# Sums over partitions in a two-model transformer kernel: from a one-column TensorE product to VectorE's block turn and row sums

## The reference

```python
for l in range(DEPTH):                                  # DEPTH = 2
    mod = jax.nn.silu(c) @ w_ada[l] + b_ada[l]          # (1,1024) @ (1024,3072) + (3072)
    shift, scale, gate = jnp.split(mod, 3, axis=-1)
    h = x * (1.0 + scale[:, None, :]) + shift[:, None, :]
    ...
    x = layer_norm_2(ALPHA * x + (1.0 + gate[:, None, :]) * sub, ln_g[l], ln_b[l])
```

## Time and profile before

| | us |
|---|---|
| median of 3 runs (1319.64 to 1320.63) | 1320.0 |
| the profiled execution | 1319.7 |
| its span in the profile | 1317.9 |
| TensorE busy in it | 1298.7 |
| VectorE busy | 1044.3 |
| ScalarE busy | 679.9 |
| GpSimd busy | 105.7 |

### The profile page before, as it was taken

The page is one execution under the profiler, slowest core; times in us unless marked ns, Lnnn a source line. Parts: engine busy times, 40 slices in busy tenths (PEclk is TensorE's granted clock), DMA queues, the critical chain, the costliest instruction groups (busy, mean ns, idle before and its releaser), DMA issues.

```text
span 1317.9 us, 18920 instructions
## 1 busy us (share of the span) xinstructions
PE 1298.7 (99%) x6968; PEld 1095.1 (83%) x6968; DVE 1044.3 (79%) x1689; ACT 679.9 (52%) x1101; POOL 105.7 (8%) x153
## 2 busy tenths in 40 slices
PE   9999999999999999999999999999999999999997
PEld 7788888788888888888887888888889998798995
DVE  6688778887888777878788887888767798966987
ACT  6444444744544444444537435444445767457672
POOL 1011100011011001101010011111000000000000
PEclk9999999999999999999999999999999999999999
DMA  8988856527888857888756349888656463464630
GB/s 266 341 268 281 265 186 208 145 95 240 273 270 270 258 191 233 274 267 274 231 168 215 102 155 326 270 300 271 204 180 191 140 221 129 144 215 132 192 129 33
DMA packets 218093, 281.73 MB, mean 214 GB/s; under 512 B 19793, under 2 KB 159185, under 8 KB 217489
## 3 DMA queue, kind: packets, MB, share of 16 engines
q1 hardware_dynamic: 183248, 223.12, 52.3%
q0 software_dynamic: 11712, 40.60, 9.2%
q10 hardware_dynamic: 23040, 16.79, 4.0%
HBM read 271.00 MB, written 9.46 MB: 213 GB/s over the span
## 4 chain that ended last, share of the span: by engine, by line
PE 88%; DVE 6%; DMA 3%; ACT 1%; issue 1%; SPq 1%; DVEq 0%; ACTq 0%
PE ps L836 27%; PE ps L838 26%; PE ps L837 26%; PE ps L920 3%; DMA w_raw<-in_ffn_w_gu 3%; DVE w_lo L1364 2%; PE ps L1070 2%; PE ps L1105 1%; PE ps L1131 1%; DMA w_raw<-in_w_in 1%; DVE few_first L1393 1%; DVE y L1392 1%; PE ps L1039 0%; PE ps L1117 0%; ACT w_hi L1162 0%
## 5 line engine op out<-in xcount | busy, mean ns | idle before, releaser
L1364 DVE TENSOR_TENSOR w_lo<-w_raw,w_hi 128x1024 fp32r<-128x1024 f32 (+2 forms) x420 | 495.4, 1212 | 73.5 <-ACT w_hi L1162 71.1
L1162 ACT ACTIVATE w_hi<-w_raw 128x1024 fp32r<-128x1024 f32 (+2 forms) x420 | 432.5, 1053 | 233.7 <-DMA w_raw<-in_ffn_w_gu 94.0
L836 PE MATMUL ps<-w_hi,col_hi 128*128 128x512 f32 (+2 forms) x1024 | 396.9, 388 | 3.9 <-DVE w_lo L1364 2.1
L838 PE MATMUL ps<-w_hi,col_lo 128*128 128x512 f32 (+2 forms) x1024 | 392.0, 383 | 0.0
L837 PE MATMUL ps<-w_lo,col_hi 128*128 128x512 f32 (+2 forms) x1024 | 391.7, 383 | 0.0
L836 PEld LDWEIGHTS ps<-w_hi,col_hi 128*128 128x128 f32 x1024 | 192.5, 188 | 47.8 <-DVE w_lo L1364 4.1
L838 PEld LDWEIGHTS ps<-w_hi,col_lo 128*128 128x128 f32 x1024 | 192.4, 188 | 38.6
L837 PEld LDWEIGHTS ps<-w_lo,col_hi 128*128 128x128 f32 x1024 | 192.6, 188 | 34.9
L836 PE MATMUL ps<-w_hi,lat_hi 128*128 128x512 f32 (+2 forms) x544 | 208.8, 384 | 0.0
L838 PE MATMUL ps<-w_hi,lat_lo 128*128 128x512 f32 (+2 forms) x544 | 206.5, 380 | 0.0
L837 PE MATMUL ps<-w_lo,lat_hi 128*128 128x512 f32 (+2 forms) x544 | 206.3, 379 | 0.0
(11 more groups left out here) (153 smaller groups left out, 1171.6 us busy)
## 6 DMA issues: line engine op xcount, KB each, us to landing
w_raw<-in_ffn_w_gu SPq DMA_DIRECT2D x352, 256.0 KB, 4.9
w_raw<-in_w_in SPq DMA_DIRECT2D x108, 512.0 KB, 4.6
w_raw<-in_ffn_w_down SPq DMA_DIRECT2D x88, 512.0 KB, 5.5
mod<-in_w_ada POOLq DMA_DIRECT2D x32, 768.0 KB, 6.9
w_raw<-in_w_out SPq DMA_DIRECT2D x24, 512.0 KB, 4.5
hidden_blocks<-arena ACTq DMA_DIRECT2D x32, 256.0 KB, 5.7
arena<-hidden_blocks ACTq DMA_DIRECT2D x128, 64.0 KB, 4.2
norm_g<-in_ln_g POOLq DMA_DIRECT2D x8, 512.0 KB, 4.1
```

What stands on the lines that cost most here:

```text
L836: pe.matmul(dst, a_hi, b_hi, start=start, stop=False)
L838: return pe.matmul(dst, a_lo, b_hi, start=False, stop=stop)
L1162: act.activation(half_of(w_hi[j], n, h), half_of(raw[j], n, h), ACT.Copy).then_inc(hi_ready, 1)
L1364: tt(half_of(w_lo[j], n, h), half_of(raw[j], n, h), half_of(w_hi[j], n, h).bitcast(F32), ALU.subtract)\
```

## The change

The sum over the 128 partitions is no longer a product on TensorE. `modsplit` and `spread` are gone. Instead:

- `modturn` (VectorE, at the place of `modsplit`): a block transpose of `ada_sum`, each 32x32 block in itself, and a sum along the rows of 32. After it, partition 32a + t holds for column 32b + t the sum over the 32 partitions of group a, as six values b (`ada_part`).
- `modmove` (ScalarE, at the place of `spread`, one round later): four copies of 32 partitions x 6 that bring the four groups to partitions 0 to 31, side by side (`ada_parts`).
- `modrow` (VectorE): one sum over the four parts and the bias, which lies beside them as a fifth. It stands at another place: behind the down product of its round, just ahead of `modturn`, where before it stood ahead of `modsum`. GpSimd's part of it moves with it in the list.
- The row is now 32 partitions x 6 values, and so the bias is loaded and the result stored in single values of 4 bytes.

```diff
     for r in range(2, ROUNDS):
         jobs += gu(r, 0)[:1] + stored(r - 1) + gu(r, 0)[1:] + by_pe(r - 1) + parts(r - 2)
         if r > 2:
-            jobs += [("spread", s, r - 3), ("modrow", s, r - 3)]
+            jobs += [("modmove", s, r - 3)]
         if r < 2 + MOD_STEPS:
             jobs += [("modsum", s, r - 2)]
         jobs += gu(r, 1)[:1] + moved(r - 1) + gu(r, 1)[1:] + blocks(r)
         if lag < ROUNDS - TAIL:
             jobs += down(lag, 0) + down(lag, 1)
             lag += 1
+        if r > 2:
+            jobs += [("modrow", s, r - 3)]
         if r < 2 + MOD_STEPS:
-            jobs += [("modsplit", s, r - 2)]
+            jobs += [("modturn", s, r - 2)]
...
-                elif kind == "spread":
-                    b, m = TURN[job][0]
-                    pe.wait_ge(mod_lo, at["modsplit", ("modsplit", s, job[2])])
-                    pe.wait_ge(free[b], m)
-                    pe.matmul(ps[0:1, 7, 0:2 * MOD_W], ones[:, 0:1], ada_both[:, :], start=True, stop=True).then_inc(turned[b], 1)
...
-                elif kind == "modsplit":
-                    act.wait_ge(mod_summed, at["modsum", ("modsum", s, job[2])])
-                    act.activation(ada_hi, ada_sum, ACT.Copy).then_inc(mod_hi, 1)
+                elif kind == "modmove":
+                    act.wait_ge(mod_folded, at["modturn", ("modturn", s, job[2])])
+                    if at["modmove", job] > 1:
+                        act.wait_ge(mod_row, at["modmove", job] - 1)
+                    for a in range(4):
+                        act.activation(ada_parts[:, a, :], ada_part[32 * a:32 * a + 32, :], ACT.Copy).then_inc(mod_moved, 1)
...
-                elif kind == "modsplit":
-                    dve.wait_ge(mod_hi, at["modsplit", job])
-                    tt(ada_lo, ada_sum, ada_hi.bitcast(F32), ALU.subtract).then_inc(mod_lo, 1)
+                elif kind == "modturn":
+                    nth = at["modturn", job]
+                    dve.wait_ge(mod_summed, at["modsum", ("modsum", s, job[2])])
+                    dve.transpose(ada_turned, ada_sum.rearrange("p (b t) -> p b t", t=32)).then_inc(mod_turned, 1)
+                    dve.wait_ge(mod_turned, nth)
+                    if nth > 1:
+                        dve.wait_ge(mod_moved, 4 * (nth - 1))
+                    dve.tensor_reduce(ada_part, ada_turned, AX_X, ALU.add).then_inc(mod_folded, 1)
                 elif kind == "modrow":
-                    b, n = TURN["spread", s, job[2]][0]
                     dve.wait_ge(bias_in, at["bias_in", ("modsum", s, job[2])])
-                    dve.wait_ge(turned[b], n + 1)
-                    steps.wait(tt(ada_row, ps[0:1, 7, 0:MOD_W], ada_bias, ALU.add))
-                    tt(ada_row, ada_row, ps[0:1, 7, MOD_W:2 * MOD_W], ALU.add).then_inc(mod_row, 1)
-                    dve.wait_ge(mod_row, at["modrow", job])
-                    dve.sem_inc(free[b], 1)
+                    dve.wait_ge(mod_moved, 4 * at["modmove", ("modmove", s, job[2])])
+                    dve.tensor_reduce(ada_row, ada_parts.rearrange("p a b -> p b a"), AX_X, ALU.add).then_inc(mod_row, 1)
...
-                pool.dma_start(ada_bias, t["b_ada_2"][l, cols].partition_broadcast(1)).then_inc(bias_in, 16)
+                pool.dma_start(ada_parts[:, 4, :], t["b_ada_2"][l, cols].rearrange("(b t) -> t b", t=32),
+                               allow_slow_non_contiguous=True).then_inc(bias_in, 16)
...
-                    pool.dma_start(mod_rows[l, cols].partition_broadcast(1), ada_row).then_inc(mod_stored, 16)
+                    pool.dma_start(mod_rows[l, cols].rearrange("(b t) -> t b", t=32), ada_row,
+                                   allow_slow_non_contiguous=True).then_inc(mod_stored, 16)
```

More of the change, by code:

```diff
@@ L408, in turn_banks_of @@
     kind, s = job[:2]
-    return {"xt": ((job[-1] + (job[2] if s == 0 else 0)) % 2 if kind == "xt" else 0,), "ht": (0,), "spread": (1,), "tr": (0, 1), "turn": (0, 1),
+    return {"xt": ((job[-1] + (job[2] if s == 0 else 0)) % 2 if kind == "xt" else 0,), "ht": (0,), "tr": (0, 1), "turn": (0, 1),
             "trret": (job[-1] % 2,) if kind == "trret" else (), "trlat": (job[-1] % 2,) if kind == "trlat" else (),
@@ L515, in count_jobs @@
             COUNT.add("y_ready", (s, job[2], job[3]))
-        if kind in ("latent", "sq", "rope", "rot", "idx", "idxw", "ropeA", "ropeK", "modsum", "modsplit", "modrow"):
+        if kind in ("latent", "sq", "rope", "rot", "idx", "idxw", "ropeA", "ropeK", "modsum", "modturn", "modmove", "modrow"):
             COUNT.add(kind, job)
@@ L675, in build @@
         ada_sum = mod[:, KT * MOD_W:(KT + 1) * MOD_W]
-        ada_row = mod[0:1, (KT + 1) * MOD_W:(KT + 2) * MOD_W]
-        ada_bias = mod[0:1, (KT + 2) * MOD_W:(KT + 3) * MOD_W]
-        ada_both, _ = sb("ada_both", [P, 2 * MOD_W], F32R, mod_at + 4 * (KT + 3) * MOD_W)
-        ada_hi, ada_lo = ada_both[:, 0:MOD_W], ada_both[:, MOD_W:2 * MOD_W]
+        ada_turned = mod[:, (KT + 1) * MOD_W:(KT + 2) * MOD_W].rearrange("p (b t) -> p b t", t=32)
+        o = (KT + 2) * MOD_W
+        ada_part = mod[:, o:o + 6]
+        ada_parts = mod[0:32, o + 6:o + 36].rearrange("p (a b) -> p a b", a=5)
+        ada_row = mod[0:32, o + 36:o + 42]
         mod_rows = nc.dram_tensor("mod_rows", (DEPTH, MOD), F32, kind="Internal").ap()
```

4 lines of the change are left out of this document (2 added, 2 removed).

## The result

The changed kernel takes **1590.4 us** (median of 4 runs, 1585.9 to 1595.7) against 1320.0 for the kernel before, measured beside it: a ratio of **1.205, interval 1.203 to 1.207**, slower. The forecast was 1465 with a range of 1425 to 1525: the sign and the mechanism came out, the size did not. The loss is 270 us where 145 was expected. By the prediction's own sign, a landing of the store of 7 us or more, it is the small pieces that were priced too low; the landing is 7.7 us. The profiled execution took 1585.9 us, 1584.1 of it span. In the changed kernel the chunk's weights are requested at line 1740, the row is stored at 1780 and the bias requested at 1744; 1479 begins `modsum`, 1496 is `modrow`, 839 to 841 are the three passes of a product.

A forecast was written before the change was run, and what follows sets the result against it. TensorE, busy 99%, bounds the kernel before; the later modrow makes VectorE's modsum wait in a loop through memory. 1319.7 + 142 (stalls in four stages) + 4 (clock) - 1 (removed products) = 1465 us, range 1425 to 1525.

The forecast's parts named there:

- The bound and the mechanism: TensorE bounds the kernel before; the later modrow delays the chunk's weights, so modsum waits in 24 of 32 chunks.
- The formula: Loss in the four ffn stages: 4 x (L - 6.6 + 5 x (L - 7.34) - 5.3), or 24 L - 194 us.
- L: Chain from the end of modrow through store, landing and bias issue to the landed next chunk, put at 14.0 us.
- The small pieces, 0.4 us: Bias and result moving as 192 pieces of 4 bytes, not sixteen of 48, add 0.4 us to the chain.
- small pieces are slow: Rival: 192 small pieces cost 4 us more in landing and issue, L = 18, 1561 us; chance 8%.
- The store's landing at the new place, 4.64: GpSimd's wait for the stored row to land, 4.64 us, taken from the kernel before.
- The chunk's landing, 6.4: Landing of the next chunk's weights, 6.4 us, a third of the way from the median 6.9 to the least 5.3.
- The lead, 5.3 us: Time from the first splits behind modsum to TensorE's use of that weight half: 5.3 us of lateness hidden per stage.
- The clock, 4 us: Slower matmuls behind the last stall of each stage after the clock falls: 0 to 13 us in all, 4 taken.
- the lateness is not taken back: Denies the rival that VectorE recovers each round and the stall does not feed itself: 48 us, 1368 us; chance 5%.
- a clock that stays low: Rival: the clock does not return between gaps, TensorE is the bound again, 389 us more, 1709 us; chance 5%.
- the first rival: No stall: the chunk lands in time, TensorE stays the bound and gains 6.4 us, 1313 us; chance 4%.

The follow-up runs named there:

- late_only: The kernel before, with its product and 48-byte pieces, and only modrow moved to the later place: 1429.9 us, ratio 1.084.
- after_24: The changed kernel with VectorE's turn reading at a stride of six, so store and bias go in 32 pieces of 24 bytes: 1431.8 us, ratio 1.086.
- late_store_pieces: late_only with the store alone cut into 192 pieces of 4 bytes from one partition's row, VectorE's sums reordered to match: 1602.0 us, ratio 1.215.
- load_before_landing: The changed kernel, but GpSimd requests the weights of chunk c + 2 behind the store's issue and ahead of the wait for its landing: 1480.3 us, ratio 1.122.
- keep_clock: The changed kernel with spare TensorE products, 36 ahead of the wait of rounds 5 to 9 and 48 ahead of round 9's hidden-row turn: 1556.9 us, ratio 1.179.
- early_row: The changed kernel with modrow back at its old place just ahead of modsum, small pieces kept: 1326.8 us, ratio 1.0085.
- early_pieces: The kernel before, modrow at its old place, with only store and bias load cut into 192 pieces of 4 bytes: 1327.7 us, ratio 1.0065.
- load_first: The changed kernel, but GpSimd requests the next chunk's weights right behind modsum, ahead of the wait for the previous modrow and its store: 1377.5 us, ratio 1.044.
- early_24: early_row with VectorE's turn reading at a stride of six, so store and bias go in 32 pieces of 24 bytes: 1312.3 us, ratio 0.9949.
- freed_24: both_freed with store and bias in 32 pieces of 24 bytes instead of 192 of 4: 1312.2 us, ratio 0.9946.
- late_both_pieces: late_store_pieces with the bias load cut into 192 pieces of 4 bytes too: 1608.6 us, ratio 1.220.
- both_freed: load_first, with the bias also requested right behind the store's issue instead of behind its landing: 1352.0 us, ratio 1.024.

## Why the prediction was wrong, step by step

**The bound and the mechanism: right.** TensorE's chain gave way to the loop modsum, modrow, store, landing, bias, weights, landing, modsum. modsum waits in exactly 24 chunks; VectorE's part of the loop is 9.2 us to the tenth in the turn shown (1052.63 to 1061.83); there are gaps ahead of the first product behind the low halves, and the clock falls. The formula, fed with each kernel's own landings, holds over the whole range:

| kernel | issues and gaps + store wait + chunk = L | by the formula | further terms | measured loss |
|---|---|---|---|---|
| late_only | 2.6 + 2.5 + 7.3 = 12.4 | 103 | two sums 12 | 110 |
| after_24 | 2.7 + 2.1 + 7.7 = 12.5 | 106 | | 113 |
| the changed kernel | 2.67 + 7.87 + 7.9 = 18.4 | 248 | bias 23 | 270 |
| late_store_pieces | 2.7 + 7.5 + 8.0 = 18.2 | 242 | two sums 19, bias 19 | 283 |
| load_before_landing | 2.1 + 0 + 11.7 = 13.8 | 137 | bias 25 | 161 |

The sum is within 7 us of each. The tighter lead, below, would add 12 to all five and put the sums up to 17 us above the measured loss, so a part of the close fit is luck. The loop and its factor of 24 hold; what failed first is L.

**The small pieces, 0.4 us: the step that failed.** I scaled from the load of c, 1,024 pieces that landed in 5.5 us, and took a fifth of the difference, by the number of pieces (192 to 1,024). That row was a poor neighbour on two counts. It is a read from DRAM, and the term on the path is a write to DRAM: in keep_clock the same 192 pieces of 4 bytes land in 2.3 us as the load of the bias and in 7.1 us as the store. And nothing showed that the excess grows in proportion to the number. The runs show 2.0 to 7.4 us for the store alone at the same place (late_only, late_store_pieces), and 7.7 to 1.6 back again (the changed kernel, after_24): 5.4 to 6.1 us, 130 to 146 us of time. The rival "small pieces are slow" was the case that came true, with 8% and a price of 4 us. L came out at 18.4 where it said 18, and that is partly luck: the pieces cost more than its 4 us, and the rest of the chain less than was taken. Its time, 1561, lacks the bias. What spoke for giving it more was in the prediction itself: it said that no row showed a store in such pieces, and its price was then bounded from above by rows of a load.

**Number or size of the pieces.** The prediction took the number of pieces to be what would matter, since by the Trainium skill ("DMA: Bandwidth & Descriptors", Specifications) 48 and 4 bytes both fall under the 512 below which a transfer is done as read-modify-write. 16 pieces of 48 bytes landed in 2.0 us, 32 of 24 in 1.6 and 192 of 4 in 7.2 to 7.7 at the later place. Being under 512 bytes is thus not enough to make a store slow. Whether the number or the size does it is not shown: both change together, and no run holds one of them fixed.

**The store's landing at the new place, 4.64: too long by 2.** In late_only it is 2.5 a time. At the later place the store falls into a stall, when less is under way: over the landings of its 32 stores the DMA engines are busy 0.33 in late_only and 0.87 in the kernel before (medians of windows of 2.0 and 4.3 us). A landing read in a full round did not hold there. I had argued so for the chunk ("fewer rounds in a given time") and not for the store.

**The chunk's landing, 6.4: too short.** 7.3 to 7.9. The argument for going below the median of 6.9, that the DMA engines have less to do, fails: they have less to do over a round, but not during this load, when they are full (1.07 in the window above, 1.00 to 1.06 over three such loads in the kernel before). Why the load takes longer than 6.9 us in late_only, at 0.94 to 0.96, stays open. Of the difference 0.2 to 0.6 us is the small pieces (7.7 in after_24 and 7.3 in late_only against 7.9). The errors of the store and of the chunk cancel in part: without small pieces L is 12.4 to 12.5 where I had 13.6, and the range given covers the 1430 of late_only.

**The lead, 5.3 us.** For the first product behind modsum it holds. But a tighter reader stood in round 10: the turn of the hidden rows of round 9 (`ht`, line 923), which needs a hidden product that stands behind modsum, and waits 50.4 us in 4. The kernel before, VectorE and TensorE at that place:

```profile
935.04 0.41 DVE L1453 SCALAR_TENSOR_TENSOR arena<-arena,ps 128x256 f32<-128x256 f32 x1
```

```profile
937.68 0.60 PE L920 MATMUL ps<-ident,arena 128*128 128x128 f32 x4
```

That is 937.68 - 935.45 = 2.2 us. I had looked only at the parts of the hidden blocks and taken them to be no tighter; this reader is, by about 3 us a stage. It is also the largest of TensorE's added waits in early_row (7.3 us in 4) and early_pieces (4.3 in 4), which lose time with waits of modsum of only 1 to 2 us; the kernel before has none there. In late_only the one-column product is one more such reader: it waits 39.3 us in 21 for `modsplit`, which now stands behind modrow.

**The bias in round 10: missing.** 23.0 us in 4 waits. The bias is requested behind the same landing as the weights, and I had followed only the weights. In load_first it is the second loop.

**The clock, 4 us: not settled.** The clock falls behind the gaps and comes back. In the turn shown, behind a gap of 4.41 us, TensorE's products start 0.43 us apart (1058.91, 1059.34), and soon 0.23 apart again (1062.00, 1062.23). TensorE's busy time rose from 1298.7 to 1354.3 us although 32 products are gone; how much of that stood on the path is not shown. keep_clock is 33 us faster, but moved the transfers too, and the sums in the table above reach the measured loss without a term for the clock. So my 0 to 13 us is neither confirmed nor refuted; spare products long enough to hold the clock and short enough not to end the round were not tried.

**The other rivals: out.** modsum waits in 24 chunks, so there is a stall. In rounds 4 to 9 modrow follows modrow by 24 to 30 us, not by 16.5, so the lateness is not taken back: the stall does feed itself. The clock returns within the round, and the time is not the 1709 of a clock that stays low.

**The removed products, 6.4 us: right.** They could not be seen in the changed kernel; early_24 and freed_24 gain 6.4 to 6.5 us, on 1312 where the first rival had 1313. **VectorE's and ScalarE's new work: right,** no cost; VectorE's sums are 0.19, 0.36 and 0.35 us, against 0.2 and twice 0.352 taken.

## What to carry to other kernels

Before a wait is placed later in an in-order queue, follow everything that the other queues have behind it, and read each reader of the late data, not the first one: a loop through memory turns one microsecond into as many as it has turns. When data is rearranged between engines, choose the order of the elements by the transfer at the end; a stride in VectorE's read made its turn 0.16 us longer (0.51 against 0.355), on an engine with time to spare, and turned 192 pieces into 32. And where no row shows a form of transfer, its bound is not the nearest row of another direction: let the range reach as far as the rival that names it.

## What the runs showed of the hardware

- A store of 768 bytes to DRAM by GpSimd's queue lands in 1.6 us as 32 pieces of 24 bytes (after_24), 2.0 as 16 of 48 (late_only), and 7.2 to 7.7 as 192 of 4 (late_both_pieces, late_store_pieces, the changed kernel), at the same place of the program. At the old place it is 3.7 (early_24), 4.3 (the kernel before), and 8.2 to 8.5 (early_pieces, early_row).
- With 192 pieces it takes 6.7 us even when the DMA engines are nearly idle (keep_clock, 0.03 busy in that time), while a load of 192 such pieces lands in 2.3 us (median) in the same run.
- Such a store slows what travels beside it. With it the 256 KB weight blocks landed in 5.6 to 6.2 us median rather than 4.6 to 5.0, and the 512 KB ones at the later place in 7.8 to 9.0 rather than 5.6 to 5.9. The exception is keep_clock, where they landed in 4.7 and 5.7 beside the same pieces; its spare products moved their requests, and what in that helped is not shown. In both_freed, where VectorE waited for neither of the small transfers, the pieces cost 40 us (1352.0 against 1312.2).
- The page does not show it as load: DMA packets are 218,093 before and 218,092 after, and the DMA share of the span falls. It is seen only in the times to landing.
- The bias load's landing follows its surroundings more than its own cut: 48-byte pieces 1.8 us (late_only) and 5.6 (late_store_pieces), 4-byte pieces 2.3 (keep_clock) and 5.9 (the changed kernel).
